# Gather, combine, residual, mean of squares and the following norm as one block, each token tile on its own

## The reference, cut to what matters

```python
hid = jax.nn.silu(hg) * hu * gates[:, :, None]     # top-2 of 32 experts for each token
out = jnp.einsum('tef,efd->td', hid, w_down)       # sum of a token's two expert rows, weighted
# then, in the trunk:
x = x + gate * out                                 # gate from adaLN: one column per prompt, one per sample row
# before the mixer of the next layer (even -> odd):
h = rmsnorm(x, g) * (1.0 + scale) + shift
# after the last layer:
y = rmsnorm(x, final_g)                            # x * rsqrt(mean(x*x) + 1e-6) * g
```

## Time and profile before

| what | us |
|---|---|
| median of 3 runs | 1963.88 |
| lowest, highest of them | 1952.72, 1969.66 |
| the profiled execution's own time | 1975.91 |
| its span, from the first to the last instruction | 1974.2 |
| PE, DVE, ACT, POOL busy in the span | 1488.5, 697.6, 458.7, 225.1 |

### The profile page before, as it was taken

How to read it: one execution, slowest core, us unless ns; L and a number is a source line. 1 busy time by engine, 2 the same in 40 slices (tenths; PEclk the granted TensorE clock), 3 DMA queues, 4 the chain that set the end, 5 groups by cost and what they waited for, 6 DMA issues and landing times. The chain is left out here.

```text
span 1974.2 us, 25279 instructions
## 1 busy us (share of the span) xinstructions
PE 1488.5 (75%) x10118; PEld 1071.7 (54%) x10118; DVE 697.6 (35%) x1247; ACT 458.7 (23%) x798; POOL 225.1 (11%) x322
## 2 busy tenths in 40 slices
PE   3699789845599887569759888814996958988852
PEld 0699544421399743369535544413996935544421
DVE  2422165632225366743341111145235361111116
ACT  1322255520124352222301110122223221101012
POOL 2000033200000043400011110021002001101010
PEclk7799899977799687779869999956998968999985
DMA  6122487469322320511559999840222196999962
GB/s 262 30 92 71 169 348 271 178 249 380 103 85 86 136 85 0 181 37 50 225 229 393 387 391 398 327 132 25 91 86 67 43 366 243 387 391 398 391 219 95
DMA packets 133568, 399.59 MB, mean 202 GB/s; under 512 B 15826, under 2 KB 67666, under 8 KB 110674
## 3 DMA queue, kind: packets, MB, share of 16 engines
q1 hardware_dynamic: 114354, 359.01, 48.4%
q10 hardware_dynamic: 11488, 21.24, 3.0%
q0 software_dynamic: 7616, 17.84, 2.9%
HBM read 368.72 MB, written 37.19 MB: 206 GB/s over the span
## 5 line engine op out<-in xcount | busy, mean ns | idle before, releaser
L2554 PE MATMUL ex_gups<-ex_gu,ex_he 128*64 128x256 f32 x2048 | 257.3, 409 | 60.5 <-DMA ex_gu<-in_moe_w_up 57.4
L2554 PEld LDWEIGHTS ex_gups<-ex_gu,ex_he 128*64 128x64 f32 x2048 | 153.3, 147 | 145.9 <-DMA ex_gu<-in_moe_w_up 64.5
L2599 DVE TENSOR_TENSOR ex_hid<-ex_sg,ex_gups 128x128 f32<-128x128 f32 x64 | 18.4, 288 | 316.3 <-ACT ex_sg L2623 316.3
L225 PE MATMUL sc_ps<-h_hi,sc_hi 128*128 128x272 f32 x384 | 111.9, 291 | 22.4 <-PEq L2075 22.4
L2572 PE MATMUL ex_yps<-ex_dn,ex_hid_t 128*64 128x512 f32 x512 | 123.9, 605 | 0.9 <-issue 0.9
L2532 POOL DMA_INDIRECT ex_hg<-h_rows,route_tok x64 | 60.2, 941 | 532.2 <-PE ex_trps L2544 423.3
L225 PE MATMUL sc_ps<-h_hi,sc_w_r 128*128 128x272 f32 x384 | 112.3, 293 | 0.0
L225 PE MATMUL sc_ps<-hT_r,sc_hi 128*128 128x272 f32 x384 | 111.6, 291 | 0.0
L225 PE MATMUL xbcz_ps<-mixT_r,xbcz_hi 128*128 128x272 f32 x320 | 93.6, 293 | 16.2 <-DVE xbcz_w_r L322 16.2
L225 PE MATMUL xbcz_ps<-mixT_r,xbcz_w_r 128*128 128x272 f32 x320 | 93.8, 293 | 0.0
L225 PE MATMUL xbcz_ps<-hT_r,xbcz_hi 128*128 128x272 f32 x320 | 93.2, 291 | 0.0
(11 more groups left out here) (449 smaller groups left out, 3225.4 us busy)
## 6 DMA issues: line engine op xcount, KB each, us to landing
ex_gu<-in_moe_w_gate SPq DMA_DIRECT2D x64, 1024.0 KB, 24.2
ex_gu<-in_moe_w_up SPq DMA_DIRECT2D x64, 1024.0 KB, 26.8
ex_dn<-in_moe_w_down SPq DMA_DIRECT2D x64, 1024.0 KB, 26.4
ada_rest_w<-in_ada_w SPq DMA_DIRECT2D x40, 1024.0 KB, 6.7
as_pages<-in_cache_kT SPq DMA_DIRECT2D x32, 512.0 KB, 6.2
as_pages<-in_cache_v SPq DMA_DIRECT2D x32, 512.0 KB, 5.5
y_rows<-ex_yo ACTq DMA_DIRECT2D x128, 128.0 KB, 7.0
qkv_w<-in_mix_w_in SPq DMA_DIRECT2D x12, 1024.0 KB, 5.3
```

Of the source, the lines that this page charges most:

```text
L225: last = nc.tensor.matmul(ps[:, h, 0:HALF], w[:, j, f], x(j)[:, cols], start=(j == 0 and n == 0), stop=(j == kt - 1 and n == 2))
L2554: last = nc.tensor.matmul(gu_ps[64 * q:64 * q + 64, :, :], he[n % 2][:, j, :], ex.gu[n % S][:, :, j, q * P:(q + 1) * P], start=(j == 0), s ...
L2599: nc.vector.tensor_tensor(hid[:, :], sg[:, :], gu_ps[:, 1, :], ALU.mult).then_inc(done["hid"], 1)
```

## The change

`phase_combine` takes over the residual and the norm that follows it, in one block; `phase_residual` is gone, and `phase_norm` is no longer called in these two places. A tile's transposed rows are no longer copied to `res`: DVE multiplies them by the gate and adds them to `xT` straight from PSUM (eight operations of 128 columns a tile), with two PSUM buffers. ACT squares the whole finished tile (128x1024) at once, PE sums the squares of a tile by eight products with a column of ones, the 1/sqrt runs on a token-major 128x4 and 32x1 array, and PE spreads it back over partitions (`bc`), which the scaling reads from PSUM. Scale and shift are folded into three operations a feature tile: DVE scales (L2936), ACT adds the shift and rounds into `h_hi` (L2875), DVE forms the rest (L2941).

In layer 0 the two `sc_w` loads stand at the head of SP's list in this block, beside the gather; the split of the first of them is taken from POOL and stands at the head of ACT's list (high part) and of DVE's list (low part). `k.recycle()` now stands in `moe`, between the experts and the combine: in layer 0 it has moved there, in layer 1 there was none in this place.

```diff
+            @block.sync
+            def _(sp):
+                if slots:
+                    slots.load(sp)
...
+            @block.tensor
+            def _(pe):
+                def turn(t):
+                    a, m = TOK[t]
+                    pe.wait_ge(s["sm"], t + 1)
+                    if t >= 2:
+                        pe.wait_ge(s["res"], t - 1)
+                    for j in range(KT):
+                        last = nc.tensor.transpose(tr_ps[t % 2][:, j, 0:m], y[0:m, t, 0, j * P:(j + 1) * P],
+                                                   k.ident[0:m, 0:m])
+                    last.then_inc(s["tr"], 1)
+
+                def mean(t):
+                    m = TOK[t][1]
+                    pe.wait_ge(s["squared"], t + 1)
+                    for j in range(KT):
+                        last = nc.tensor.matmul(stats[t // 4][0:m, t:t + 1], sq[:, t % 2, j, 0:m], k.ones[:, 0:1],
+                                                start=(j == 0), stop=(j == KT - 1), skip_group_check=True)
+                    last.then_inc(s["mean"], 1)
...
+                for t in range(TT):
+                    turn(t)
+                    if t:
+                        mean(t - 1)
+                mean(TT - 1)
+                spread(range(4), 0)
+                spread((4,), 1)
+
             @block.scalar
             def _(act):
+                nc.scalar.preload_act_table_set("sqrt_and_others")
+                if slots:
+                    act.wait_ge(k.w_ready[0], 16 * (k.rounds + 1))
+                    nc.scalar.activation(slots.hi[0][:, :, :], slots.raw[0][:, :, :], ACT.Copy).then_inc(k.w_hi[0], 1)
+
+                def square(t):
+                    a, m = TOK[t]
+                    act.wait_ge(s["res"], t + 1)
...
+                    nc.scalar.activation(sq[:, t % 2, :, 0:m], k.xT[:, :, a:a + m], ACT.Square).then_inc(s["squared"], 1)
+
                 for t, (a, m) in enumerate(TOK):
                     act.wait_ge(gathered[t], 32)
                     nc.scalar.activation(y[0:m, t, 0, :], y[0:m, t, 0, :], ACT.Copy,
-                                         scale=r.weight[0:m, 0, t:t + 1]).then_inc(sc, 1)
+                                         scale=r.weight[0:m, 0, t:t + 1]).then_inc(s["sc"], 1)
+                    if t:
+                        square(t - 1)
+                square(TT - 1)
...
+                if slots:
+                    dve.wait_ge(k.w_hi[0], k.rounds + 1)
+                    V.tensor_tensor(slots.lo[0][:, :, :], slots.raw[0][:, :, :], slots.hi[0][:, :, :], ALU.subtract)\
+                     .then_inc(k.w_lo[0], 1)
...
+                def residual(t):
+                    a, m = TOK[t]
+                    dve.wait_ge(s["tr"], t + 1)
+                    if t < 4:
+                        for j in range(KT):
+                            ins = V.scalar_tensor_tensor(out=k.xT[:, j, a:a + m], in0=tr_ps[t % 2][:, j, :],
+                                                         scalar=k.mod[:, m0 + j, 0:1], in1=k.xT[:, j, a:a + m],
+                                                         op0=ALU.mult, op1=ALU.add)
...
+                for t in range(TT):
+                    merge(t)
                     if t:
-                        pe.wait_ge(ev, t)
+                        residual(t - 1)
+                residual(TT - 1)
...
+    phase_route(k, layer, r, ahead)
+    phase_experts(k, layer, r, ex)
+    k.recycle()
+    return r
...
-        moe(k, 0)
-        k.recycle()
         with ExitStack() as c:
+            r = moe(k, 0, c)
...
-                phase_norm(k, "n2", 1, 0, h_hi, slots)
+                phase_combine(k, 0, r, h_hi, slots)
...
-        moe(k, 1)
-        phase_norm(k, "n4", None, 0)
+        with ExitStack() as c:
+            phase_combine(k, 1, moe(k, 1, c))
```

More of the change, by code:

```diff
@@ L2035, in samples @@
         V.tensor_tensor(hs, hs, b, ALU.add).then_inc(self.sample, 1)
[L2038 to L2053, removed]
 def phase_short_conv(k, gT, g_lo, h_hi, slots, next_w):
@@ L2811, in _ @@
+                if not final:
+                    for j in range(KT):
+                        act.wait_ge(s["scaled"], j + 1)
+                        nc.scalar.activation(h_hi[:, j, 0:TP], k.hT[:, j, 0:TP], ACT.Identity,
+                                             bias=k.mod[:, shift0 + j, 0:1]).then_inc(s["high"], 1)
+                    act.wait_ge(s["samples"], 1)
+                    nc.scalar.activation(h_hi[:, :, TP:T], k.hT[:, :, TP:T], ACT.Copy).then_inc(s["high"], 1)
             @block.vector
@@ L2833, in phase_combine @@
[L2833 to L2838, removed]
-        with ExitStack() as c:
-            ex = Experts(k, layer, c)
-            def ahead(sp):
-                r.load(k, sp)
-                ex.load_ahead(sp)
-            phase_route(k, layer, r, ahead)
-            phase_experts(k, layer, r, ex)
-        phase_combine(k, layer, r)
+                own = Chain(dve, s["own_d"])
+                V = nc.vector
@@ new lines, in _ @@
+                scale(0)
+                scale(1)
+                dve.wait_ge(s["spread"], 2)
+                hs = k.hT[:, :, TP:T].rearrange("p k (b q) -> p k b q", q=NQ)
+                wide = lambda m: k.mod[:, m:m + KT, 1:NC9].unsqueeze(3).to_broadcast([P, KT, NB, NQ])
+                own.step(V.tensor_tensor(k.hT[:, :, TP:T], k.xT[:, :, TP:T],
+                                         bc[:, TP:T].unsqueeze(1).to_broadcast([P, KT, TS]), ALU.mult))
+                own.step(V.tensor_tensor(hs, hs, wide(scale0), ALU.mult))
@@ new lines, in _ @@
+                V.tensor_tensor(hs, hs, wide(shift0), ALU.add).then_inc(s["samples"], 1)
+                for j in range(KT):
+                    if j + 2 < KT:
+                        scale(j + 2)
+                    dve.wait_ge(s["scaled"], j + 1)
+                    low(j)
+                dve.wait_ge(s["samples"], 1)
+                dve.wait_ge(s["high"], KT + 1)
+                V.tensor_tensor(k.hT_r[:, :, TP:T], k.hT[:, :, TP:T], h_hi[:, :, TP:T], ALU.subtract).then_inc(s["low"], 1)
@@ L2851, in build, with moe, ahead @@
+                dve.wait_ge(s["low"], KT + 1)
+        if slots:
+            slots.ahead = True
+def moe(k, layer, ctx):
+    r = Routing(k, ctx, layer)
+    with ExitStack() as c:
+        ex = Experts(k, layer, c)
+        def ahead(sp):
+            r.load(k, sp)
+            ex.load_ahead(sp)
+        phase_route(k, layer, r, ahead)
+        phase_experts(k, layer, r, ex)
+    k.recycle()
+    return r
 def build(nc, io):
```

88 lines of the change are left out of this document (69 added, 19 removed).

## The result

| | before | after |
|---|---|---|
| median, first set of runs (4 and 4) | 1965.29 | 1948.59 |
| ratio of that set, 95% interval | | 0.9889, 0.985 to 0.9927 |
| ratio of a second set, 95% interval | | 0.9877, 0.9839 to 0.9915 |
| profiled execution, its span | 1975.91, 1974.2 | 1952.4, 1950.7 |
| layer 0: last row store issued to the norm's end | 75.15 | 60.78 |

The forecast of 1950 was a saving of 13.9 us. The medians of the first set differ by 16.7; the two ratios, on 1963.88, give 21.8 and 24.2; the profiled executions differ by 23.5, of which the two stretches hold 14.4 and 8.5. So the time was met, but the saving was larger than forecast, at or past the upper bound of 22.0, and nearly all of the difference is in layer 0: 14.4 us where 6.2 were forecast (layer 1: 8.5 for 7.7).

A forecast was written before the change was run, and what follows sets the result against it. The prediction saw two stretches bound by a chain of hand-offs, no engine busy throughout; savings of 6.2 us in layer 0 and 7.7 in layer 1, sum 13.9, take the median of 1963.88 to 1950, range 1940 to 1962.

The forecast's parts named there:

- the upper bound of 22.0: Whole kernel: largest saving in us, with the first load landing at 8.9 and both tails at 6.5; median 1942.
- the clear: Semaphore clearing, now ahead of the gather in both layers: costs 0.96 us before each block starts.
- The load's landing: Layer 0's first weight load beside the gather: lands 14.0 us after the first gather, bounds 8.9 and 17.7.
- The rule of the Trainium skill: DMA queues: an engine drains a whole packet, some 9 to 17 descriptors, before changing queue; first load 6 to 7 us.
- The weights go first: Rival, layer 0's loads: many weight packets per gather packet, residual 0 at 17.2, 18.4 us saved, 1945.5; chance 0.24.
- the forecast's sharing from the start: Layer 0's gather and load queues: equal packet counts, each 1 KB weight packet waiting for a 4 KB gather packet; 0.70.
- The turn: Tile loop: ACT's order makes residual, square, scale and merge take 5.9 us a tile; three turns 17.7.
- cut the tie: Tile loop without ACT's order tying scale t+1 to residual t-1: turn 3.5 us, each layer 7.2 shorter.
- TensorE becomes the bound: Rival, PE's sums of squares ahead of the next transposes: 7.9 us a sum, 26 us slower, 1990; chance 0.06.
- The tail: After residual 3: last square, sums of tiles 3 and 4 and the spread take 8.0 us, range 6.5 to 11.5.
- Layer 1: Layer 1's merged block, without weight loads: ends 47.05 us after the gather against 54.7, 7.7 us saved.
- the prediction's own sign: Layer 0's block: a cast early in the block and turns of 5.9 would leave the total right by luck only.

The follow-up runs named there:

- e5: Changed kernel, but layer 0's weight loads start only when tile 0's gathered rows have landed; layer 0 73.40 us against 60.78.
- e3: Changed kernel, but layer 0's loads wait for the gather's last tile, cast and subtraction moved later in their lists; layer 0 58.44 us against 60.78.
- e1: Changed kernel, but ACT takes each tile's square one scale later; layer 0 58.55 us against 60.78, layer 1 from block start 44.27 against 46.89.
- e8: Changed kernel with ACT's squares one scale later, single-pass float32r sums and late weight loads; layer 0 53.74 us, ratio to before 0.9779.
- e9: Version with later squares, single-pass sums and late loads, but POOL casts and subtracts the weights; layer 0 51.51 us, ratio to before 0.9768.
- e4: Changed kernel, but layer 0's loads wait for a semaphore behind tile 0's gathers in POOL's list; layer 0 61.40 us against 60.78.
- e10: Version with later squares, single-pass sums, late loads and POOL's split, but the split waits for the last residual; layer 0 50.39 us, ratio to before 0.9763.

## Why the prediction was right and where it was wrong

*What bounds it, and the clear.* This was right. The gather starts 6.78 and 9.94 us after the last row store, before 5.92 and 8.85: 0.86 and 1.09 for the clear, forecast 0.96.

*The load's landing: wrong.* The forecast was 14.0 with bounds of 8.9 and 17.7, and 5.2 came. The sharing was read rightly from the earlier trace rows: one packet for one, in e5 too. The step that failed is the next one. The earlier trace rows showed a gather that had its first packets 3.8 us after its issue behind loaded queues, and the prediction turned this delay into packets, of which 1 KB ones would pass in a fifth of the time. The delay is nearer to a time than to a count of packets: 4.7 us behind 1 KB packets here, 3.3 for loads behind 4 KB rows (e5), 1.7 for a gather with nothing ahead (e3), while the packets that passed an engine meanwhile were 88 here (1406 on 16 engines) and 16 in e5. More than the first load's 1040 went alone, so even the lower bound was passed. A second term was put at nothing: POOL's first gather is issued 0.78 us after the loads. With the row's 3.8 us kept whole, these 0.78 added and the 1.05 that loads alone took to their first packet taken off, the loads have 3.5 us, 70 packets of the prediction's 50 ns on an engine, where the first load needs 65. Why a queue starts late beside a loaded one was not tried.

The rule of the Trainium skill that was weighed there (DMA: Bandwidth & Descriptors, section Queues, rings and completion order) gave an estimate of 6 to 7 us, nearest to the 5.18, but not for a reason that the trace bears out. The estimate gives the gather a single row at each change of queue, where the rule as it was quoted would give it 9 to 17 descriptors too, and so would not put the weights first. And equal counts over a microsecond leave open in what portions an engine takes them; the packets' starts and ends in the trace do not. From 1297 to 1299 a load's packet began 1 to 4 ns ahead of the end of a gather row 201 times, and a gather row ahead of the end of a load's packet 200 times; two of one queue met like this 33 and 46 times, about as often as any two packets 4 ns further off. So an engine took one traced packet of each queue in turn, and the rule does not hold here if a traced packet is a descriptor; whether it is, no run shows.

*What followed from it.* *The weights go first*, given 0.24, is what happened, and not the forecast's sharing from the start, given 0.70; it came by the late start that the prediction gave in its favour, and not by many weight packets for one gather packet. The cast started 4.4 us after the first gather, before even the 6 to 9 that were named as this rival's sign. The rival's arithmetic was near: tile 0 9.5 us after the gather (11.6 forecast), residual 0 at 15.0 (17.2). The forecast's chain behind the landing was right as well: it put 7.65 us from the landing to residual 0, and e5, where the landing does decide, shows 7.49. Against the forecast's 62.1 from the first gather, layer 0 ended at 54.0: residual 0 6.7 earlier, turns 0.8, tail 0.2, scaling 0.4, together 8.1.

*The turn.* It was forecast at 5.9 and measured at 5.62, for the reason named (ACT's order: e1's first distance without it is 3.27). Wrong was what it would be worth to cut the tie, 7.2 us a layer: e1 gave 2.2 and 2.6. *TensorE becomes the bound* was priced right as a threshold (up to 3.9 us a sum the turn holds; it was 3.57) and did not come true, but it stood 0.1 us behind, which the forecast, with sums near 2.1, did not see.

*The tail.* It was forecast at 8.0 and measured at 7.76, with wrong terms that cancel. 8.0 less the square leaves 6.85 for 40 records, 2.74 for each of two sums and 1.37 for the spread (the 2.1 for a sum that was named as a sign is another price). A full sum took 3.57 at the lower clock, tile 4's, of 32 columns, 0.94 (4.51 less 3.57), and the spread 2.11 to the start of the scaling.

*Layer 1.* From the gather it was forecast at 47.05 and measured at 46.13; no step was off by more than 1 us.

*The total.* That 1950 stands so near 1948.59 is luck, by the prediction's own sign: the cast came early and the turns near 5.9. The numbers agree because the first set's medians differ by less than the ratio and the stretches say. By the stretches the forecast's saving was 9 us too small, for the landing above all.

## What to carry to other kernels

In these runs a transfer that was issued beside another cost what the order of their first packets made it: before sharing is priced, read from the trace how long each queue takes from issue to first packet with the other loaded, keep that as a time, and see which engine issues first. Where a loop's turn is explained by one engine's order, put the busy time of every other engine in that turn beside it: the next bound may stand a tenth of a microsecond behind, and then only both edits together pay. And work that is moved to another engine has to be looked at for whom it holds up there (the cast in ACT's list in e8, POOL's subtraction in e9, and the same subtraction in the kernel before).

## What the runs showed of the hardware

*A queue's late start.* A gather's first packet came 1.7 us after its issue alone (before, e3), 4.7 behind loads issued 0.78 us earlier, and 3.3 with loads issued 0.38 us later (e4). The loads' first packet came 1.05 us after their issue alone, and 3.3 behind a gather in flow (e5).

*POOL and DVE.* DVE's sums of two tensors in SBUF waited for the end of POOL's subtraction (3.25 and 0.97 instead of 0.43 us, both ending 0.28 after it; 4.83 instead of 0.73 in the kernel before), while operations with an operand in PSUM kept their length beside it (two scalings in 1.41, in e10 and, without POOL's subtraction, in the changed kernel). This agrees with the Trainium skill (SBUF — State Buffer, section SBUF: two separate sides), which has the two engines share a pair of ports that the first to start holds for its whole instruction, where DVE reads two SBUF inputs and GpSimd reads SBUF. The other direction shows as well, though not always: POOL's gather issue beside DVE's subtraction took 2.99 instead of 0.99 and ended 0.87 after it (timeline above), but one beside a merge in layer 1 took 0.92. In all traces here the order tells these apart: an issue that began before such a merge or subtraction, or up to 0.07 us after its start, kept its 0.91 to 0.99; one that began 0.10 us or more after it ended 0.78 to 0.96 after DVE's end.

*TensorE's clock.* Over 19 us in which PE was busy nine tenths of the time with sums of a single column and transposes, the granted clock stayed at 0.50, the level of 1.2 GHz. In e4, after sixteen transposes back to back and 1.71 us of waiting, a sum ran at a mean of 0.84, between the level of 1.2 GHz (0.50) and that of 2.4 (1.00), and took 2.23 us instead of 3.57. The next rows are stretches of e4, the transposes and that sum:

```profile
1303.88:1307.48 3.60, 3.60 (x16) 3.27 (x16) 2.73 (x8) 0.00 (x0) 0.79 (x1) 0.53 1.04 397
1309.19:1311.42 2.23, 2.23 (x16) 2.15 (x16) 1.11 (x1) 0.99 (x1) 0.00 (x0) 0.84 0.07 12
```
